# Spreading the inverse row sums of a softmax: GpSimd copies and two transposes in place of four float32 products, in a hybrid decoder step

## The reference

```
def fox_attend(q, fq, pq, k, v, fk, pk):
    s = jnp.einsum('bqhd,bkhd->bhqk', q, k).astype(jnp.float32) * (HEAD_DIM ** -0.5)
    s = s + jnp.swapaxes(fq, 1, 2)[..., :, None] - jnp.swapaxes(fk, 1, 2)[..., None, :]
    s = jnp.where(pq[:, None] >= pk[None, :], s, -jnp.inf)
    p = jax.nn.softmax(s, axis=-1)
    return jnp.einsum('bhqk,bkhd->bqhd', p.astype(v.dtype), v)
```

## Time and profile before

| | us |
|---|---|
| three timed runs | 679.54, 681.82, 683.3 |
| span of the profiled execution | 678.7 |
| PE busy | 656.1 (97%) |
| DVE busy | 385.9 (57%) |
| ACT busy | 266.4 (39%) |
| POOL busy | 144.4 (21%) |
| PE on the chain that ended last | 86% |

### The profile page before, as it was taken

One profiled execution on the slowest core, in us unless ns is written; L12 is line 12 of the kernel. 1 busy time (PEld: TensorE's weight loads), 2 busy tenths in 40 slices (PEclk: granted clock), 3 DMA queues, 4 the chain that ended last, 5 costly groups with the idle time before them and its releaser, 6 DMA issues.

```text
span 678.7 us, 13245 instructions
## 1 busy us (share of the span) xinstructions
PE 656.1 (97%) x5183; PEld 564.7 (83%) x5183; DVE 385.9 (57%) x709; ACT 266.4 (39%) x486; POOL 144.4 (21%) x164
## 2 busy tenths in 40 slices
PE   6999999999999999999999998999999999999996
PEld 6989999898999889999999975776667755688884
DVE  5854916572455315149999766445443568554633
ACT  6636443111111245221213354645555666332321
POOL 3181112111111011223221140123222201121210
PEclk9999999999999999999999999999999999999998
DMA  7512103131100032345120364468666723113132
GB/s 208 172 43 63 32 2 76 39 87 32 33 8 27 5 85 71 93 133 155 32 62 1 106 178 147 119 177 256 178 205 187 221 108 109 48 62 125 63 125 93
DMA packets 59735, 67.29 MB, mean 99 GB/s; under 512 B 14156, under 2 KB 49883, under 8 KB 59673
## 3 DMA queue, kind: packets, MB, share of 16 engines
q1 hardware_dynamic: 54505, 51.37, 25.7%
q0 software_dynamic: 5168, 15.08, 7.5%
HBM read 57.71 MB, written 8.68 MB: 98 GB/s over the span
## 4 chain that ended last, share of the span: by engine, by line
PE 86%; DVE 7%; ACT 3%; issue 2%; DMA 1%; SPq 0%; DVEq 0%; ACTq 0%
PE PS L1925 14%; PE PS L1926 14%; PE PS L1927 14%; PE PS L1814 4%; PE PS L1815 4%; PE PS L1816 4%; PE PS L2214 4%; PE PS L2196 3%; PE PS L2171 3%; PE PS L2101 3%; PE PS L2149 3%; PE PS L2114 2%; DVE rows_odd L1693 1%; DVE YF L1572 1%; PE PS L2240 1%
## 5 line engine op out<-in xcount | busy, mean ns | idle before, releaser
L1925 PE MATMUL PS<-xh,wh 128*128 128x368 f32 x576 | 196.0, 340 | 0.3 <-DVE RA L1512 0.3
L1926 PE MATMUL PS<-xl,wh 128*128 128x368 f32 x576 | 190.2, 330 | 0.0
L1927 PE MATMUL PS<-xh,wl 128*128 128x368 f32 x576 | 189.7, 329 | 0.0
L649 POOL TENSOR_TENSOR wl<-wr,wh 128x1024 fp32r<-128x1024 f32 x23 | 59.7, 2597 | 263.1 <-ACT wh L1023 263.1
L1925 PEld LDWEIGHTS PS<-xh,wh 128*128 128x128 f32 x576 | 108.2, 188 | 4.1 <-issue 1.6
L1926 PEld LDWEIGHTS PS<-xl,wh 128*128 128x128 f32 x576 | 108.2, 188 | 0.9
L1927 PEld LDWEIGHTS PS<-xh,wl 128*128 128x128 f32 x576 | 108.2, 188 | 0.0
L1552 DVE RECIPROCAL RA<-RA 128x1104 f32<-128x1104 f32 x8 | 56.4, 7053 | 4.8 <-ACT RA L1169 4.6
L628 DVE TENSOR_TENSOR wr<-wr,small 128x1024 f32<-128x1024 f32 x24 | 35.9, 1495 | 35.3 <-DMA wr<-in_w_in_dram 35.2
L1814 PE MATMUL PS<-woh,yh 128*128 128x512 f32 x128 | 50.5, 395 | 0.0
L1816 PE MATMUL PS<-woh,yl 128*128 128x512 f32 x128 | 50.2, 392 | 0.0
(11 more groups left out here) (330 smaller groups left out, 1093.3 us busy)
## 6 DMA issues: line engine op xcount, KB each, us to landing
wr<-in_w_in_dram SPq DMA_DIRECT2D x24, 512.0 KB, 3.9
kpage<-in_cache_fox_k_dram SPq DMA_DIRECT2D x64, 192.0 KB, 3.0
RA<-in_cache_fox_v_dram POOLq DMA_DIRECT2D x32, 192.0 KB, 3.5
pagesB<-in_cache_fox_v_dram POOLq DMA_DIRECT2D x32, 192.0 KB, 3.7
YF<-in_x_prompt_dram SPq DMA_DIRECT2D x8, 512.0 KB, 7.0
xres<-in_x_prompt_dram SPq DMA_DIRECT2D x8, 512.0 KB, 3.7
out_y_p_dram<-zout SPq DMA_DIRECT2D x16, 256.0 KB, 2.1
wo_raw_a<-in_w_out_dram SPq DMA_DIRECT2D x6, 512.0 KB, 6.3
```

Of the source, the lines that this page charges most:

```text
L649: eng.tensor_tensor(low, wr[:, c % 2, :, 0:m], wh[:, c % 2, :, 0:m].bitcast(F32), ALU.subtract).then_inc(wlo_done, 1)
L1925: pe.matmul(out, high, xh[:, k, cols], start=(k == 0), stop=False)
L1926: pe.matmul(out, high, xl[:, k, cols], start=False, stop=False)
L1927: ins = pe.matmul(out, low, xh[:, k, cols], start=False, stop=(k == KT - 1))
```

## The change

GpSimd writes the inverses out 64 times into two 128x128 views of gstate (slots 0 and 2), one for each of the quarter's two query tiles, the two heads side by side. PE then turns each with one plain transpose. The semaphore wide_done takes the place of inv_done on PE, and that of ring_full in DVE's wait before it overwrites inverses of the pair of heads before. ACT's waits on inv_done stay. GpSimd overwrites the two views for a quarter only when PE has turned those of the quarter before.

```diff
+        inv_wide = [gstate[:, a_, :, :].rearrange("p i d -> p (i d)") for a_ in (0, 2)]
...
+            def widen(p, q):
+
+                n_q = QUARTERS.index((p, q))
+                g.wait_ge(inv_done, n_q + 1)
+                if n_q:
+                    g.wait_ge(ring_full, RI[("sum",) + QUARTERS[n_q - 1]] + 1)
+                for a_ in range(2):
+                    ins = g.tensor_copy(inv_wide[a_].rearrange("p (i d) -> p i d", i=2),
+                                        row_inv[:, 2 * q + a_, :, None].to_broadcast([P, 2, HD]))
+                ins.then_inc(wide_done, 1)
+
             load_bias(1)
             for kind, key in PLAN:
                 if kind == "L":
                     load_values(*key)
+                elif kind == "I":
+                    widen(*key)
...
                 if p:
-                    dve.wait_ge(ring_full, RI["sum", p - 1, q] + 1)
+                    dve.wait_ge(wide_done, QUARTERS.index((p - 1, q)) + 1)
                 two = slice(2 * q, 2 * q + 2)
                 dve.reciprocal(row_inv[:, two, :], row_sum[:, two, :]).then_inc(inv_done, 1)
...
-                pe.wait_ge(inv_done, QUARTERS.index((p, q)) + 1)
-                for i in range(2):
-                    for a_ in range(2):
-                        ins = pe.matmul(out[64 * i:64 * i + 64, P * a_:P * a_ + P],
-                                        row_inv[:, 2 * q + a_, i:i + 1].to_broadcast([P, HD]), ident[:, :],
-                                        start=True, stop=True)
+                pe.wait_ge(wide_done, QUARTERS.index((p, q)) + 1)
+                for a_ in range(2):
+                    ins = pe.transpose(out[:, P * a_:P * a_ + P], inv_wide[a_], ident[:, :])
                 ins.then_inc(ring_full, 1)
```

More of the change, by code:

```diff
@@ L434, in build @@
         exp_done, pv_done, inv_done = sem("exp_done"), sem("pv_done"), sem("inv_done")
+        wide_done = sem("wide_done")
         pt_dve, pt_act = sem("pt_dve"), sem("pt_act")
```

## The result

The changed kernel takes 683.45 us (median of 6 runs, 682.65 to 684.64), the kernel before 681.16 us in the runs beside it (6 runs, 679.54 to 683.3). The ratio is 1.0038, with a 95% interval of 1.0022 to 1.0053: 2.3 us or 0.4% slower. The forecast was 679.5, with 677.7 to 683.2 as the range; the time lies 0.25 us above the range, and the sign is wrong. The forecast stood on the first three runs of the kernel before, 681.82; its 2.3 us off the 681.16 of all six would be 678.9.

The account below looks back on a forecast made before the run. PE's time was taken to bound the kernel. Ten quarters saving 0.37 us each (3.7), less 1.4 lost in quarter 0, gave 2.3 us off 681.82: 679.5 us, range 677.7 to 683.2.

Parts of the forecast that it names:

- What bounds it: PE's time, busy 656.1 of 678.7 us, bounds the kernel; POOL's own order is the thing to check.
- Quarter 0's wait: At the first spreading, POOL's copies stand behind DMA issues; PE waits some 2.7 us, a net loss of 1.4.
- The clock: PE's granted clock: such transposes already stand in a stretch at 1.00, so 24 more got no price.
- The saving per quarter: Spreading on PE: 0.59 us for 8 records becomes 0.22 for two transposes, saving 0.37 us a quarter.
- My low end: Low end of the spreading's saving: 0.28 us a quarter, with the transpose pair at 0.31, the dearest row.
- The ten quarters that pass it on: All quarters but 0 and 10 pass the spreading's saving on along PE: 10 x 0.37 = 3.7 us.
- they move with them: PE's waits on PT and scores after the spreading are round trips PE's transposes start, so they come earlier too.
- Quarter 10: Saving lost there: four transposes behind the spreading, PE stands 0.67 us for ACT's exponentials, which don't depend on it.
- Rival B: Saving not passed on: PE's waits on PT and scores follow DVE and ACT; 0.8 us gain, 681.0; chance 0.17.
- The sum: Whole kernel: -3.7 us saved plus 1.4 lost in quarter 0 gives -2.3 us, from 681.82 to 679.5.
- Rival A: First POOL copy in quarter 0 dear, awaiting DMA landings or code: 683.2 at 3.7 us, 680.8 at 1.28; chance 0.13.
- The range: Kernel time 677.7 to 683.2 us, from PE saving more than the starts show to a dear first copy.

## Why the prediction was wrong

- **What bounds it.** Right: PE's time, and POOL's order as the danger.
- **Quarter 0's wait.** Right in place, cause and size. I forecast copies of 0.29 us; they take 0.30. I forecast a wait of some 2.7 us and a net loss of 1.4; the wait is 2.6, and with PE kept at work the loss is 1.38.
- **The clock.** This is the first step that failed. I priced the idle time as idle time alone, "So quarter 0 loses 1.4 us net", and looked at the clock only as a matter of transposes. The idle time of 2.6 us was followed by over 3 us at 1.2 GHz, which cost 1.7 us more. The Trainium skill, "TensorE: Matmul & The Clock Gate", section "Part 1: The HAM clock gate", says that the gate follows how busy PE has been. Three traces here agree with it (two with the idle time, one with it filled); the falls at 160 to 170 us, with PE busy 5.00 of 5.00 us, it doesn't account for. I should have asked that rule of the new wait.
- **The saving per quarter.** The second step that failed, a term mis-sized: 0.37 forecast, 0.21 measured (0.29 in quarter 11). I took the price of transposes inside a stream of transposes; in this place the pair has 0.16 us beside it. My low end, 0.28 from the dearest pair in the trace, was not low enough either, since I read it up to the next start and not from the last start ahead.
- **The ten quarters that pass it on.** The third step that failed. Six pass it on. "they move with them" was wrong for quarters 1, 3, 5 and 7, where ACT's copy to PT stood behind exponentials that began ahead of the spreading. Quarter 10 was right. Rival B named this mechanism and gave it 0.17, but of its five quarters (2, 5, 6, 9 and 10) only 5 and 10 were so.
- **The sum.** The forecast was 2.3 us faster. The cheaper saving takes 1.5 off it (10 quarters give 2.2 in place of 3.7), the four quarters that give it back 0.8, and the clock 1.7: 1.7 us slower, as by the trace. The two errors in the saving alone bring it to nothing (1.37 - 1.38); the clock makes it slower and takes it out of the range.
- **Rival A.** Its place was right, its mechanism wrong. The copies begin within 0.01 us of the end of the DMA issues, so neither a landing nor a load of code stands ahead. The first-call load that the Trainium skill, "GPSIMD Engine Reference", section "Instruction dispatch", names for a freshly loaded routine is not seen for this copy. The time came out just past A's 683.2 all the same, by other causes: that is no point for A.
- **The range** had both ends of the terms of cost and saving, and no term for the clock. Its upper end was rival A's, so that it missed by 0.25 us only is luck.

## What to carry to other kernels

When a change adds a wait to an engine at full load, look up where the helper's in-order queue stands at that moment, at every place, the first one above all: an engine that is 21% busy kept PE idle for 2.6 us once, and that turned the result. Price idle time on PE twice, once as time and once as what the clock may take behind it. Here moving the helper's first copies ahead of its DMA issues was the difference between slower and faster, 3.1 us by the traces. And a saving on the bounding engine is passed on only if what it then waits for is released by work behind the saving, not by a chain that began ahead of it.

The best version is the one with the copies first and the sampled exponentials behind the copy to PT: 0.9955 (0.994 to 0.997) of the kernel before, 3.3 us.

## What the runs showed of the hardware that I had not expected

- 2.60 and 2.59 us of idle PE were each followed by some 3 us at the 1.2 GHz level; 1.54 us of it at the same place was not, in one trace each.
- The granted clock also fell at 160 to 170 us in three of ten traces without any idle time of PE there (0.71 over 165 to 170 with PE busy 5.00 of 5.00 us), which cost 1.5 us each, and at 235 to 245 us in one, which cost 3.1.
- A copy of 128x128 float32 numbers with a broadcast input takes GpSimd 294 to 304 ns in each of 24, and two follow each other in 0.54 us.
- One more 128x128 float32 transpose costs 0.11 us of PE, the same as in a stream, but a pair of them between float32 products and the next transposes costs 0.16 beside that: the product ahead takes 0.10 longer than it does ahead of another float32 product.
